# A recurrent state update moved ahead of the routing ranks, and two more moved up in VectorE's program

## The reference, cut to what matters

```python
def _layer(x, c, ...):
    mod = silu(c) @ w_mod + b_mod                    # shift, scale, gate, twice
    u = rmsnorm(x) * (1 + sc1) + sh1
    m, buf, h_last, s_last = _mixer(u, ...)          # RG-LRU group | 4 retention heads
    x = x + g1 * rmsnorm(m)
    u2 = rmsnorm(x) * (1 + sc2) + sh2
    return x + g2 * rmsnorm(_moe(u2, ...)), buf, h_last, s_last

def _retention(q, k, v, s0):                         # returns each head's state matrix:
    s_last = chunk_decay * s0 + k^T (w_state * v)    # 128 x 128 per sequence and head

def _moe(u, ...):                                    # 16 experts in 4 groups
    p_group = softmax(u @ w_rg + b_rg);   g = argmax(p_group)
    p_e = softmax(the 4 logits of group g);  top_w, top_i = top_k(p_e, 2)
    gates = p_group[g] * top_w / sum(top_w)          # two experts a token
    h = silu(u @ w_g[e]) * (u @ w_u[e])              # 1024 -> 256
    out = sum over e of gates[e] * (h @ w_d[e])      # 256 -> 1024
```

## Time and profile before

| what | value |
|---|---|
| median of three runs | 541.12 us (540.18 to 541.88) |
| the profiled execution: time, span | 539.75 us, 537.5 us |
| PE busy | 518.3 us, 96% of the span |
| DVE, ACT, POOL busy | 259.3, 151.2, 155.0 us |
| chain that ended last | PE 82%, DMA 8%, DVE 5%, issue 2%, ACT 1% |
| mean granted clock of TensorE | 0.993 of full speed |

### The profile page before, as it was taken

The page is one execution under the profiler, slowest core; times in us unless marked ns, Lnnn a source line. Parts: engine busy times, 40 slices in busy tenths (PEclk is TensorE's granted clock), DMA queues, the critical chain, the costliest instruction groups (busy, mean ns, idle before and its releaser), DMA issues.

```text
span 537.5 us, 7583 instructions
## 1 busy us (share of the span) xinstructions
PE 518.3 (96%) x2798; PEld 322.0 (60%) x2798; DVE 259.3 (48%) x759; ACT 151.2 (28%) x293; POOL 155.0 (29%) x166
## 2 busy tenths in 40 slices
PE   7999999999999999999999999878999999999994
PEld 6777755554455454557544444557887768668841
DVE  3543465543024223342633276576746766663247
ACT  6332497721122222232222315410100111011132
POOL 3016000116000000000310020336777677777310
PEclk8999999999999999999999999999999999999998
DMA  9999997899900000007931022969998999999574
GB/s 289 357 330 353 340 312 312 306 388 370 333 4 1 0 0 1 1 1 284 382 112 64 39 66 87 382 190 402 364 355 282 365 370 364 365 377 368 124 197 179
DMA packets 47417, 126.50 MB, mean 235 GB/s; under 512 B 6654, under 2 KB 19358, under 8 KB 41234
## 3 DMA queue, kind: packets, MB, share of 16 engines
q1 hardware_dynamic: 30912, 99.36, 50.1%
q0 software_dynamic: 11408, 22.05, 15.0%
q10 hardware_dynamic: 5058, 4.58, 2.5%
HBM read 116.48 MB, written 17.30 MB: 249 GB/s over the span
## 4 chain that ended last, share of the span: by engine, by line
PE 82%; DMA 8%; DVE 5%; issue 2%; ACT 1%; POOL 0%; ACTq 0%; SPq 0%; POOLq 0%; DVEq 0%
PE psum L816 78%; DMA f_dram<-arena,add_tok 5%; PE psum L819 3%; DMA u_dram<-arena 2%; DVE arena L2386 1%; DVE x L2391 1%; DMA arena<-f_dram 1%; DMA hy<-in_c_sample_dram 1%; ACT arena L1502 1%; DVE arena L2187 0%; ACT L1502 0%; POOL f_dram L785 0%; DVE arena L2333 0%; ACT hy L1502 0%; POOL uT L774 0%
## 5 line engine op out<-in xcount | busy, mean ns | idle before, releaser
L816 PE MATMUL psum<-ring,uT 128*128 128x512 f32 (+1 forms) x384 | 126.5, 523 | 0.0
L816 PEld LDWEIGHTS psum<-ring,uT 128*128 128x128 f32 (+1 forms) x384 | 56.7, 173 | 60.0 <-issue 55.7
L1502 ACT ACTIVATE arena<-psum 128x512 f32<-128x512 f32 (+6 forms) x80 | 35.7, 476 | 168.2 <-PE psum L816 150.9
L816 PE MATMUL psum<-uT,ring 128*128 128x288 f32 x256 | 64.9, 411 | 0.1
L816 PEld LDWEIGHTS psum<-arena,ring 128*128 128x128 f32 x512 | 58.5, 192 | 5.9 <-issue 3.9
L816 PE MATMUL psum<-arena,ring 128*128 128x128 f32 x512 | 59.2, 276 | 2.7 <-DVE arena L2187 1.8
L754 POOL DMA_INDIRECT arena<-u_dram,part_tok x52 | 53.4, 1027 | 19.9 <-issue 14.3
L816 PEld LDWEIGHTS psum<-uT,ring 128*128 128x128 f32 x256 | 47.9, 190 | 16.2 <-issue 4.0
L816 PE MATMUL psum<-ring,arena 128*64 128x256 f32 (+2 forms) x192 | 50.6, 490 | 0.0
L785 POOL DMA_INDIRECT f_dram<-arena,add_tok x26 | 41.5, 1598 | 23.1 <-DMA f_dram<-arena,add_tok 13.2
L1502 ACT ACT_TABLE_LOAD x33 | 42.3, 1283 | 3.1 <-issue 2.1
(11 more groups left out here) (260 smaller groups left out, 613.4 us busy)
## 6 DMA issues: line engine op xcount, KB each, us to landing
ring<-in_w_mod_dram SPq DMA_DIRECT2D x24, 1024.0 KB, 11.5
ring<-in_w_exp_down_dram SPq DMA_DIRECT2D x12, 1024.0 KB, 13.4
ring<-in_w_exp_gate_dram SPq DMA_DIRECT2D x11, 1024.0 KB, 9.9
ring<-in_w_exp_up_dram SPq DMA_DIRECT2D x11, 1024.0 KB, 12.5
ring<-in_w_in_dram SPq DMA_DIRECT2D x10, 1024.0 KB, 10.2
ring<-in_w_out_dram SPq DMA_DIRECT2D x4, 1024.0 KB, 6.9
uT<-in_w_exp_gate_dram SPq DMA_DIRECT2D x4, 1024.0 KB, 14.2
f_dram<-in_consts_dram POOLq DMA_DIRECT2D x2, 1536.0 KB, 17.0
```

The costliest lines, as they stand in the source:

```text
L816: return nc.tensor.matmul(out, lhsT, rhs, start=first, stop=last)
L1502: return nc.scalar.activation(out, src, func, **kw).then_inc(done, 1)
```

## The change

It has five parts. On TensorE `add_state(1)` goes ahead of the rank matmuls, where `keep_running(4, 4)` stood, and that filler goes where `add_state(1)` was; the filler `keep_running(4, 3)` ahead of `turn_first` is dropped. On ScalarE `take_state(1)` goes ahead of the second exponential of the gates, and the one-element Silu, which loads the activation table, goes behind the store of state 1, after the branch. On VectorE `new_state(2)` is run between `places()` and `numbers(1)`; `take_input(0)` is run straight after `hits(2)`, with `new_state(3)` behind it, and `orders()` after both. The code for the overflow branch on VectorE is unchanged.

```diff
@@ -1286,7 +1286,7 @@
 
 
             pe.wait_ge(s_u2Te, 2 * TILES)
-            keep_running(4, 4)
+            add_state(1)
             pe.wait_ge(s_rsel, 1)
             pe.wait_ge(s_clear, 6)
             pe.wait_ge(s_x1, TILES)
@@ -1301,7 +1301,7 @@
                 n = rows(j)
                 last = mm(bank[6][:, 0:NE], ones[0:n], sel[0:n, j], j == 0, j == TILES - 1)
             last.then_inc(s_rank, 1)
-            add_state(1)
+            keep_running(4, 4)
 
             def slot_tokens(e):
 
@@ -1442,7 +1442,6 @@
                 for e in range(1, AHEAD):
                     state_step(e + 1)
                     slot_tokens(e)
-                keep_running(4, 3)
                 turn_first()
                 for e in range(NST):
                     if paired(e):
@@ -1786,10 +1785,9 @@
 
             act.wait_ge(s_gin, 1)
             f(gx[:, :, 0:NG], gx[:, :, 0:NG], ACT.Exp, s_gexp)
+            take_state(1)
             act.wait_ge(s_gin, 2)
             f(gx[:, :, 4:5], gx[:, :, 4:5], ACT.Exp, s_gexp)
-            f(softp[:, 0, 0:1], eps[:, 0:1], ACT.Silu, s_act)
-            take_state(1)
 
             for k in range(2):
                 act.wait_ge(s_u2st[k], 16 * (4 - 2 * k))
@@ -1810,6 +1808,7 @@
             def store_second():
                 act.wait_ge(s_sold, 2)
                 store_state(1, again)
+                f(softp[:, 0, 0:1], eps[:, 0:1], ACT.Silu, s_act)
 
             def store_rest():
                 for h in range(2, NH):
@@ -2512,10 +2511,12 @@
 
                 hits(1)
                 places()
+                new_state(2)
                 numbers(1)
                 hits(2)
+                take_input(0)
+                new_state(3)
                 orders()
-                take_input(0)
                 numbers(2)
                 gate_weights()
                 dve.wait_ge(s_gw, 1)
@@ -2524,8 +2525,6 @@
                 v.tensor_tensor(out=oh[1], in0=oh[1], in1=w16(rm2), op=ALU.mult).then_inc(s_fb, 1)
                 dve.wait_ge(s_fb, 2)
                 v.tensor_tensor(out=gates[:], in0=oh[0], in1=oh[1], op=ALU.add).then_inc(s_gw, 1)
-                for h in range(2, NH):
-                    new_state(h)
                 for e in range(NST):
                     if e + AHEAD < NST:
                         hits(e + AHEAD)
```

## The result

| | before | changed |
|---|---|---|
| median, beside each other on one chip | 540.65 us (540.13 to 541.88, 4 runs) | 546.48 us (545.56 to 548.61, 4 runs) |
| ratio, 95% interval | | 1.011 (1.0075 to 1.0145) |
| profiled execution: time, span | 539.75, 537.5 us | 546.42, 544.1 us |
| mean granted clock | 0.993 | 0.987 |

The change costs 5.8 us. The direction was forecast, the size was not: 546.48 us lies above the range.

What follows compares the result with a forecast made beforehand. TensorE's own work was taken as the bound, with the gates' chain through VectorE, POOL and two DMAs meeting it near 381 us; 0 + 0 + 2.4 + 0 = +2.4 us on 541.12 gave 543.5 us, range 541.2 to 545.9.

Steps and rivals of the forecast that it cites:

- what bounds the kernel: TensorE's own work from 366.23 us, met near 381 us within some 0.2 us by the gates' chain.
- the exchange of waits: TensorE's 1.80 us wait in step 0 goes; one of about 4.5 us comes in step 1: +2.4 us.
- the order of VectorE, +2.37: With `new_state(3)` and `orders()` behind the copy, `numbers(2)` begins at 362.76 instead of 360.39, making the gates later.
- The delay of `numbers(1)`: On VectorE, `numbers(1)` starts 0.85 us later behind `new_state(2)`, bounds 0.7 and 1.2.
- The 14.89 us from the mark to the use of the gates: From VectorE turning to the next thing after the gates (363.70) to their use (378.59); assumed to hold.
- Value 0, bounds 0 and -0.1 us: TensorE behind the ranks: 1.05 in place of 1.98 us of work, hidden because the branch waits for `over`.
- the gap of 1.8 us that "let it stay up": TensorE's wait at the branch, from 350.90 in the kernel before, where the clock was seen to stay up.
- the clock's fall behind the new wait: Rival: clock falls in step 1's gap of close to 4 us, adding 1.7 us, 545.2 us; chance 0.26.
- Weights. Value 0: SyncE's late weights start 3.9 us later at no cost; bound +3.9 if the lag reached a wait.
- Some 36 us after their start: Step 3 uses the first late weight at 395.64, some 36 us after the late weights' DMAs start.
- A gates' chain in time: Rival: gates land by about 376.4 us, TensorE keeps its 2.14 us lead, 539.0 us; chance 0.08.

Runs made afterwards that it cites:

- a_pe_back: Changed kernel with TensorE's order at the ranks put back (four-matmul filler ahead of the ranks, `add_state(1)` behind): 544.98 us, ratio 1.0087.
- b_pe_only: Kernel before with only the swap of `add_state(1)` and filler on TensorE and the earlier `take_state(1)` on ScalarE: 542.73 us, ratio 1.0041.
- b_pe_fill: Kernel before with the swap on TensorE and ScalarE's part, but eight filler matmuls behind the ranks instead of four: 540.65 us, ratio 1.0000.
- b_dve_only: Kernel before with only the change's whole order on VectorE; TensorE, its fillers and ScalarE as before: 546.26 us, ratio 1.0112.
- b_gates_late: Kernel before with only the four state operations on VectorE moved ahead of the gates' computation: 543.32 us, ratio 1.0041.
- a_fill: Changed kernel with 14 more filler matmuls in step 1's wait, ahead of its slot matmuls: 545.00 us, ratio 1.0090.
- e_state_gates: Kernel before with VectorE's `new_state(2)` early, gates ahead of `take_input(0)`, `orders()` last, and the filler ahead of the transposes dropped: 546.10 us, ratio 1.0099.
- e_gates_first: Kernel before with VectorE computing the gates straight after `hits(2)`, ahead of `take_input(0)`, and `orders()` last: 548.21 us, ratio 1.0138.
- b_orders_late: Kernel before with only `orders()`, which releases the late weights, moved behind the state operations: 552.11 us, ratio 1.0206.

## Why the prediction was wrong, by its steps

**Right: what bounds the kernel, and the exchange of waits.** Two chains met near 381 us, and the one through the gates decided. The wait of 1.80 us went, one of 3.47 us came, released by VectorE's masks, at the place named.

**Right in size: the order of VectorE, +2.37.** With the clock at the branch left alone (a_pe_back), `take_out(0)` came 2.50 us later, counted from `over`. The delay of `numbers(1)` was 0.93 us for 0.85, and that of `numbers(2)` 2.47 for 2.37. The 14.89 us from the mark to the use of the gates became 14.52 (369.23 to 383.75).

**Wrong: "Value 0, bounds 0 and -0.1 us" for the 0.93 us less behind the ranks.** This is the step that failed. I asked which work waits for TensorE there, found none, and did not ask what the work itself was keeping up. It kept the clock: b_pe_only costs 1.8 us, b_pe_fill nothing. I had a row in front of me that seemed to excuse it, the gap of 1.8 us that "let it stay up"; the change lengthens this very gap, and I asked after the clock only in the new gap further on. In the changed kernel the fall made the state steps 2.39 us longer, and as `new_state(2)` had been moved up to wait for them (2.18 us idle before L2186), the delay went straight to the gates: `take_out(0)` 3.90 us later in place of 2.50.

**Wrong in weight: the clock's fall behind the new wait.** Its place and price were given, +1.7 us, measured 1.55. But it had a chance of 0.26 and was no part of the sum. Of five profiles with a wait of over 2 us in step 1 (the changed kernel, a_pe_back, b_dve_only, b_gates_late with 2.06, and a_fill), only a_fill, whose wait is filled, kept the clock. The section of the Trainium skill that I cited for it ("TensorE: Matmul & The Clock Gate", on HAM oscillation) said what happened; I let one gap that the clock had survived outweigh it.

**Right by luck: "Weights. Value 0".** The first late weight was asked for 6.51 us later, not 3.9, and this cost nothing in the changed kernel only because TensorE was late by nearly as much (5.45 us). "Some 36 us after their start" looked at the first weight, that of step 3; what comes late is those of step 10, seven steps on. The weights stream through DMA engines that hardly have a free moment until then (in the kernel before, DMA share 1.03 at 407 GB/s from 368 to 376 us, and 0.91 to 1.04 in each of the stretches of 25 us from 375 to 475). A gates' chain in time would not have saved the change: e_state_gates has it, and starves for 6.28 us.

With both falls the sum would have been +2.5 + 1.4 + 1.6 = +5.5 us, which is the passage measured; +5.8 is the time.

**What stays open.** Why the DMA to `u_dram` lands some 0.2 us later in some executions, and with it why the rest at the branch is longer, isn't settled. Nor is the rest all that decides: b_dve_only, with 2.01 us, kept its clock, and e_gates_first, with 1.79, lost it.

## What to carry to other kernels

Before real work is moved away from a place where TensorE is about to rest, ask what keeps the clock up there; the check is the granted clock of the next stretch, and the remedy, if it falls, is as much filler as was taken. Where an operation releases a long stream of DMAs through busy DMA engines, its time is the whole stream's time: look for the first wait of the consumer much later, not at the first transfer. And count an order of work by all the chains that leave it; here the one order that gained (1.5 us) runs the 1.27 us that release the weights, and the gates, first, and the outputs that nobody reads last.

## What the runs showed of the hardware

- A few tenths of a microsecond of rest went with the clock's fall. Of seven profiles with 1.51 to 1.90 us of rest at the branch one fell (e_gates_first, 1.79), of seven with 1.99 to 2.04 us six did. A fall there made 4.01 us of matmuls 5.46 to 6.65 us long.
- The small DMAs of the gates took 6.1 us (32 KB) and 6.2 us (4 KB) in the kernel before, where the DMA share was 1.02 from 364 to 371 us. In e_gates_first, where the weights were not yet asked for and the share was 0.05 from 361 to 364 us and, with these DMAs in it, 0.33 from 363.5 to 367, the same two took 2.3 and 2.0 us:

```profile
gates_dram<-gates POOLq DMA_DIRECT2D x1, 32.0 KB, 2.3
gates_dram<-gates POOLq DMA_DIRECT2D x1, 4.0 KB, 2.0
```

 So the fixed cost of about 2 us in the Trainium skill ("DMA: Bandwidth & Descriptors", on the anatomy of one DMA on the GpSimd path) holds where the DMA engines had little to do; the 4 us more came where they were busy.
- An issue on SyncE's queue takes 0.33 to 0.38 us mostly, but 8.58 us in b_orders_late at 479.44 and 8.75 us in e_gates_first at 476.08, both close to where TensorE starved, and 2.74 us at 472.54 in the kernel before. What held it isn't shown.
